# 56 instead of 48 tokens by gathered expert rows, the choice of experts begun earlier, and one comparison for both one-hots

## What is computed

```python
q = (xb @ w_q).reshape(T, 8, 2, 128)                 # the query projection, 2048 x 2048
sc = einsum('thcd,hckd->thck', q, sub_keys)          # 8 heads, 2 halves, 128 keys each
s1, i1 = top_k(sc[:, :, 0], 16); s2, i2 = top_k(sc[:, :, 1], 16)
cand = s1[..., :, None] + s2[..., None, :]           # 256 candidates for each head
best, ci = top_k(cand.reshape(T, 8, 256), 16)
idx = i1[ci // 16] * 128 + i2[ci % 16]               # 128 picks of a token, of 16384 experts
g = softmax(best)
act = gelu(einsum('td,thkd->thk', xb, u_tab[idx]))
out = einsum('thk,thkd->td', g * act, v_tab[idx])
```

## Time and profile before

| | |
|---|---|
| median of 3 timed runs | 1776.24 us (1774.4 to 1777.46) |
| the profiled execution | 1771.97 us, its span 1769.7 us |
| TensorE busy (PE) | 1744.7 us, 99% of the span |
| TensorE's weight loads (PEld) | 1655.2 us |
| VectorE busy (DVE) | 1423.8 us, 80% |
| ScalarE busy (ACT) | 931.9 us, 53% |
| GpSimd busy (POOL) | 415.8 us, 23% |
| DMA | 462.59 MB, mean 261 GB/s |
| high products u, v | 438.4 and 438.9 us busy, 2048 each |
| query projection, u stage, v stage begin | 360, 450 and 1125 us |

### The profile page before, as it was taken

One profiled execution on the slowest core, in us unless ns is written; L12 is line 12 of the kernel. 1 busy time (PEld: TensorE's weight loads), 2 busy tenths in 40 slices (PEclk: granted clock), 3 DMA queues, 4 the chain that ended last, 5 costly groups with the idle time before them and its releaser, 6 DMA issues. The chain is left out here.

```text
span 1769.7 us, 28855 instructions
## 1 busy us (share of the span) xinstructions
PE 1744.7 (99%) x10950; PEld 1655.2 (94%) x10950; DVE 1423.8 (80%) x2151; ACT 931.9 (53%) x1403; POOL 415.8 (23%) x293
## 2 busy tenths in 40 slices
PE   9999999999999999999999999999999999999997
PEld 7887778788999999999999999999999999999997
DVE  4556786575589899999999998688888888888995
ACT  5454574444456555555555545555555545555553
POOL 0002300020142133111111112023434433343341
PEclk9999999999999999999999999999999999999998
DMA  7765455678577677777777779899999999999992
GB/s 233 213 188 167 143 150 178 184 255 236 172 218 219 218 256 243 253 240 230 230 227 228 232 232 324 254 338 373 353 357 344 356 325 356 360 368 403 366 347 85
DMA packets 127138, 462.59 MB, mean 261 GB/s; under 512 B 14864, under 2 KB 14944, under 8 KB 126352
## 3 DMA queue, kind: packets, MB, share of 16 engines
q1 hardware_dynamic: 95760, 347.65, 60.5%
q0 software_dynamic: 30960, 112.64, 17.1%
q10 hardware_dynamic: 288, 0.55, 0.1%
HBM read 455.73 MB, written 5.05 MB: 260 GB/s over the span
## 5 line engine op out<-in xcount | busy, mean ns | idle before, releaser
L1641 PE MATMUL PS<-W,HI 128*128 128x416 f32 x2048 | 438.9, 354 | 1.4 <-DVE W L1222 0.8
L1601 PE MATMUL PS<-xT,HI 128*128 128x416 f32 x2048 | 438.4, 356 | 0.0
L682 ACT ACTIVATE HI<-V_RAW 128x1024 fp32r<-128x1024 f32 x256 | 271.7, 1062 | 282.6 <-PE PS L1641 151.4
L1641 PEld LDWEIGHTS PS<-W,HI 128*128 128x128 f32 x2048 | 366.1, 189 | 7.2 <-DVE OUTA L1256 1.9
L1601 PEld LDWEIGHTS PS<-xT,HI 128*128 128x128 f32 x2048 | 366.0, 189 | 2.9
L1146 DVE TENSOR_TENSOR V_LO<-V_RAW,HI 128x2048 fp32r<-128x2048 f32 x128 | 293.0, 2289 | 48.6 <-ACT HI L682 43.4
L682 ACT ACTIVATE HI<-RING_RAW 128x1024 fp32r<-128x1024 f32 x256 | 269.6, 1053 | 77.5 <-DMA RING_RAW<-u_t 72.0
L1153 DVE TENSOR_TENSOR RING_LO<-RING_RAW,HI 128x1024 fp32r<-128x1024 f32 x232 | 274.4, 1219 | 4.6 <-ACT HI L682 4.6
L819 DVE TENSOR_TENSOR LO<-RAW,HI 128x1024 fp32r<-128x1024 f32 x132 | 163.1, 1238 | 142.8 <-PE PS L1349 97.9
L1607 PEld LDWEIGHTS PS<-xT,RING_LO 128*128 128x128 f32 x2048 | 268.0, 191 | 3.7 <-DVE RING_LO L1153 2.2
L1646 PEld LDWEIGHTS PS<-W,V_LO 128*128 128x128 f32 x2048 | 269.4, 191 | 1.9 <-DVE V_LO L1146 0.8
(11 more groups left out here) (209 smaller groups left out, 1656.9 us busy)
## 6 DMA issues: line engine op xcount, KB each, us to landing
RING_RAW<-u_t SPq DMA_DIRECT2D x256, 512.0 KB
V_RAW<-peer_v SPq DMA_DIRECT2D x256, 512.0 KB
RAW<-w_in SPq DMA_DIRECT2D x80, 512.0 KB, 3.7
RAW<-w_out SPq DMA_DIRECT2D x32, 512.0 KB, 4.4
RAW<-wq_t SPq DMA_DIRECT2D x32, 512.0 KB, 4.8
x_spill<-X POOLq DMA_DIRECT2D x2, 1024.0 KB, 5.8
X1R<-x_spill POOLq DMA_DIRECT2D x8, 256.0 KB
X<-x SPq DMA_DIRECT2D x3, 512.0 KB, 8.4
```

The costliest lines, as they stand in the source:

```text
L682: nc.scalar.activation(HI[:, n % HI_SLOTS, :], raw_of(n), ACT.Copy).then_inc(top_ready, 1)
L1601: return mm(PS[:, j % S_BANKS, 0:2 * ND].rearrange("p (a t) -> p a t", a=2), HI[:, n % HI_SLOTS, kk * P:(kk + 1) * P], xT[:, k, :, 0:ND], ...
L1641: return mm(PS[:, V_BANKS[i], 0:2 * ND].rearrange("p (a t) -> p a t", a=2), HI[:, v % HI_SLOTS, i * P:(i + 1) * P], weights_of(v), start=v ...
```

## The change

- NB_ goes from 16 to 24, so 56 tokens go by gathered rows and ND is 200. A gather of part B now brings 5 picks of 24 tokens (120 of 128 partitions used, the indices of the other 8 zero), so GROUPS_B is 26 and HALVES 232. 65 halves stand in the u stage (two of three spreading steps have one, and the steps after them 1.5 on average), 167 in the v stage. Their order is now dots A, sums A, dots B, sums B, with gelu for each part.
- The choice begins in the query projection: TensorE makes the scores of a pair of heads' halves there (`pair_scores`), ACT copies them out, and VectorE does the first 12 pieces at every second unit. The pieces end in step 47 and spreading begins in step 51, with 50 batches. The loops of the query projection on ACT, VectorE and TensorE are written out. VectorE waits for the saved rows of XS before that loop.
- The one-hots are one comparison on VectorE (ONE, both indices), and the gate is multiplied in on ACT by four activations (`gates_into`), which stand ahead of `put_gates` on ACT. On VectorE `one_hots(b + 1)` now stands ahead of `apply_gates(b)`. `land` keeps its waits.
- Some tiles move (X8, ACC8, PICKED2, PK4), and POOL has low parts in 16 units instead of 24.

```diff
-NA, NB_ = 32, 16
+NA, NB_ = 32, 24
-GROUPS_A, GROUPS_B = P * NA // P, P * NB_ // P
+PICKS = PH * TOPK
+ROWS_A, ROWS_B = P // NA, P // NB_
+PB = ROWS_B * NB_
+GROUPS_A, GROUPS_B = PICKS // ROWS_A, -(-PICKS // ROWS_B)
...
+EARLY = 12
+CHOICE0 = 1
...
-SPREAD0 = 60
+SPREAD0 = PICKS_AT[1] + 2
...
-HALF_STEPS = list(range(40, SPREAD0, 3)) + list(range(SPREAD0, SPREAD_END, 2)) + list(range(SPREAD_END, NKEYS - 7))
+HALF_STEPS = sorted([j for j in range(SPREAD0 - 3, SPREAD_END) if j % 3] + list(range(SPREAD_END, NKEYS - 7))
+                    + list(range(SPREAD_END, NKEYS - 7, 2)))
...
+def half_of(k):
+
+    if k < A_SUMS:
+        return k < A_DOTS, k % A_DOTS // 2, k % 2
+    return k < B_DOTS, GROUPS_A + (k - A_SUMS) % (2 * GROUPS_B) // 2, k % 2
...
+            def pair_scores_out(q):
+
+                act.wait_ge(sc_done, q + 1)
+                nc.scalar.activation(SC[:, TILE_ORDER[0], 2 * q:2 * q + 2, :],
+                                     PS[:, 4 + q % 4, q // 4 * 2 * NKEYS:(q // 4 + 1) * 2 * NKEYS]
+                                     .rearrange("p (a b) -> p a b", b=NKEYS), ACT.Copy).then_inc(sc_out, 1)
+
+            for m in range(4, N_WQ):
+                hi(WQ0 + m)
+                if m >= 9 and m % 4 == 1:
+                    pair_scores_out((m - 9) // 4)
...
+            def gates_into(b):
+
+                act.wait_ge(compared, b + 1)
+                for i in range(TOKB):
+                    t = b * TOKB + i
+                    ins = nc.scalar.activation(ONE[:, 1, i, :], ONE[:, 1, i, :], ACT.Copy, scale=EG[:, 2, t:t + 1])
+                ins.then_inc(ones, 1)
...
+                if 0 <= j + 1 - SPREAD0 < N_BATCH:
+                    gates_into(j + 1 - SPREAD0)
                 if 0 <= j - SPREAD0 < N_BATCH:
                     put_gates(j - SPREAD0)
...
+            dve.wait_ge(xs_saved, 16)
+            for m in range(2, N_WQ + 2):
+                if m < N_WQ:
+                    lo(WQ0 + m)
+                c = (m - 3) // 2
+                if m % 2 and c >= 0:
+                    dve.wait_ge(used, WQ0 + 2 * c + 2)
+                    add_halves(QTQ[:, c, :], c % 2)
+                if m % 2 == 0 and 0 <= (m - 8) // 2 < EARLY:
+                    piece()
...
-                v.tensor_tensor(ONE1[:], IOTA[:].unsqueeze(1).broadcast_to([P, TOKB, NKEYS]),
-                                EG[:, 0, b * TOKB:(b + 1) * TOKB].unsqueeze(2).broadcast_to([P, TOKB, NKEYS]), ALU.is_equal)
-                for i in range(TOKB):
-                    t = b * TOKB + i
-                    ins = v.tensor_scalar(ONE2[:, 4 * i:4 * i + 4, :], IOTA[:].rearrange("p (q c) -> p q c", q=4),
-                                          EG[:, 1, t:t + 1], EG[:, 2, t:t + 1], ALU.is_equal, ALU.mult)
-                ins.then_inc(ones, 1)
+                t0 = b * TOKB
+                v.tensor_tensor(ONE[:], IOTA[:].unsqueeze(1).unsqueeze(1).broadcast_to([P, 2, TOKB, NKEYS]),
+                                EG[:, 0:2, t0:t0 + TOKB].unsqueeze(3).broadcast_to([P, 2, TOKB, NKEYS]), ALU.is_equal)\
+                    .then_inc(compared, 1)
...
-                if 0 <= b < N_BATCH:
-                    apply_gates(b)
                 if 0 <= b + 1 < N_BATCH:
                     assert done == [PIECES, PIECES]
                     one_hots(b + 1)
+                if 0 <= b < N_BATCH:
+                    apply_gates(b)
                 if b >= 0:
                     land(j)
```

250 lines of the change are left out of this document (126 added, 124 removed).

## The result

The changed kernel took 1826.33 us (median of 4 runs, 1818.87 to 1843.52), the kernel before 1775.32 beside it (4 runs, 1772.08 to 1777.46): a ratio of 1.0303, 95% interval 1.0228 to 1.0377. It is 3.0% slower; the forecast was 0.6% slower, 1786, with a range up to 1806. The profiled execution took 1825.0 us (span 1823.2), 53.5 us of span more than the one of before. Ratios are taken without runs in the slower state that some executions fall into, and can differ a little from the quotient of the medians.

What follows compares the result with a forecast made beforehand. TensorE was taken as the bound, with VectorE and DMA close behind. Columns -27.3, batches -1.7, spreading +33 and gathers +6 gave +10.0 on 1771.97, so 1782.0; against the timed median, 4.3 higher, 1786 us, range 1760 to 1806.

Steps and rivals of the forecast that it cites:

- The columns: TensorE, u and v stages: 16 columns fewer in 4096 high products save 27.3 us; 8 fewer in low products, nothing.
- The gap rule: TensorE's isolated gap of N / 2.4 + 2.5 ns; would shorten the low products too, making the sum 13.7 us better.
- The batches: Spreading in the u stage: two batches fewer (52 to 50) at 0.83 us each save 1.7 us.
- The spreading step: u stage: landing waits for ACT's scalings and `put_gates`, so a step takes 6.33 us against TensorE's 5.61; loss 33 us.
- the lead: TensorE's head start in the spreading steps: a batch's gates are ready before its spread wants them, so 2.9 us are absorbed.
- The choice in the query projection: 12 of 82 pieces move into the query projection, with VectorE busy 41 of 50 us there; cost taken as nothing.
- The end of the u stage: Gathered halves at 1.5 per step, VectorE at 4.57 of 4.72 us; 0 to 5 us for late loads, taken as 0.
- The gathers in the v stage: Round trip of 10.06 us against 10.1 available: 0.05 us per pair, 6 us in all; bounds 0 and 39.
- Rival 3: The gather round trip sets the v stage too: at 10.8 us, 39 instead of 6, time 1819; at 10.4, 1796; chance 0.14.

Runs made afterwards that it cites:

- The swap: The changed kernel with `put_gates` ahead of the four scalings on ScalarE in a spreading step, not behind them: 1803.68 us, ratio 1.0183.
- the cut chain: The changed kernel; VectorE applies gates before comparing for the next batch, ScalarE copies gates and low half out before scaling: 1784.75 us, ratio 1.0057.

## Why the forecast was wrong

- **The columns** (-27.3, upper end 13.7 more): measured -34. The high products saved what was taken. The low ones, taken to be at a floor, fell by 0.01 us per 8, and the unit by 0.066 instead of 0.053. The gap rule that the forecast weighed (the Trainium skill, TensorE: Matmul & The Clock Gate, Back-to-back issue gap) would have made it 0.080, as an estimate; the rows lie halfway.
- **The batches** (-1.7): two are gone, and nothing in the runs speaks against their 0.83 us each.
- **The spreading step** (+33): right in mechanism, 9 us short in size. ACT's scaling costs 0.295 us start to start (taken 0.29), the step 6.43 (taken 6.33) against 5.59 (taken 5.61): 0.84 x 50 = 42. Of the 9 us, 6 are the longer step and 3 the lead. The lead is used up after three steps (TensorE first waits at 727.3); it was taken off at 2.9 us, and the mean of 6.43 already has it. The swap and the cut chain show that it is the order and nothing else.
- **The choice in the query projection** (0): 0 by its own run, 93.1 us with and without. VectorE is busy 39.56 of 50 us there, where 41 was forecast. The query stage's +4.3 us are about 3 of pair scores that moved there from the u stage and a slow first unit (its first 7 high products took 3.08 us at 360.62, where the window of 355 to 365 us had a granted clock of 0.83). But the early choice has a price that the forecast did not see, further on: it moves the gathers' dense stretch.
- **The end of the u stage** (0, bounds 0 to 5): 7.0 us of stalls and 2.8 at the slower clock behind the last spread, where before had none, so +10. The forecast added up VectorE's load there (4.57 of 4.72) and asked neither what ScalarE waits for nor what the gathers do at 1.5 per step. ScalarE's gelu, in order ahead of the high parts, waited for the last dot product (a stall of 2.95 us and the slow clock), and VectorE's low parts came late, since VectorE itself waited 9.9 us for rows.
- **The gathers in the v stage** (+6, bounds 0 and 39): this is the step that failed. The stage lost 25.7 us in stalls and 8.0 at the slower clock against 3.3 before, so +30. The forecast read a round trip of 10.06 us off one place of the trace of before, compared it with the 10.1 that the change leaves, found the two about equal and took the small end, 0.05 us per pair. The reading was near the mean, 10.1 us before and after. The step from it to the price was wrong: a mean round trip that equals the spacing is not just covered, since a single one takes from 8.8 to 11.9 us (eight of ten in the changed kernel) and the long ones make VectorE wait. Part of the scatter is the issue on GpSimd, 0.94 us or up to 3.0 behind VectorE's operation in course, part the landing (6.2 to 8.1 us from the end of the issue, again eight of ten). Before, 11.6 us of spacing covered most of it. And VectorE, at 4.39 of 4.716 us by the forecast's own sum, has too little time in hand to catch up, so its waits reach TensorE: 49.7 us for rows of the sums, 21.2 us of TensorE's stalls for value weights behind them. Rival 3 had this as its mechanism (gathers set the v stage, deciding above 10.1 us) at a chance of 0.14, and gave it as an alternative to the spreading loss, while the two add up: 1786 with 30 for 6 and 42 for 33 is 1819, and the end of the u stage (+10) and the columns (-7) bring it to 1822, the measured 1826 less what has no name.

Of the Trainium skill, SBUF — State Buffer (Who interferes with whom) says that an operation of VectorE with two inputs in SBUF and an instruction of GpSimd that reads SBUF exclude each other for the whole of it. The trace agrees for gathers, which read their list there: the issue at 1311.52 ends 0.83 us after the low pair that had begun before it. Whether an issue in turn holds up VectorE these rows don't show. The same section infers that such an operation does not hold up the writing of descriptors for a transfer; for plain transfers no run here was made to show it, for gathers the rows above speak against it.

What stays open: why gathers into 64 or 96 partitions make both queues and the issues slower, and how much of the changed kernel's spread of run times (1818.87 to 1843.52) comes from stalls that tip the clock. How large the cost of the gelu's place is, when the same lines take between 130.7 and 135.2 us from run to run. Of the 53.5 us some 5 in the v stage have no name. Whether the changed kernel's v stage is bound to lose 30 us each time isn't known either: the same lines took 647.2, 646.5, 646.1 and 656.5 us in four traces.

## What to carry to other kernels

A ring with n places asks for a round trip under n times the spacing, and that holds for its long trips, not for its mean: read many of them, and how they scatter, before pricing a smaller spacing, and ask whether the engine that waits has time in hand. Here a spacing equal to the mean cost 30 us, and 10% fewer transfers in the stage gave it back. When work moves to another engine, follow what is queued behind it there: the same operations in another order were worth 41.6 us. And a mean over long and short steps says nothing where the short ones can't give back.

## What the runs showed of the hardware

- A gather's issue on GpSimd takes 0.94 us alone and otherwise ends 0.82 us after VectorE's operation in course (126 of 135 in the v stage), so up to 3.0 behind a low pair of 2.28 us; some lose more than one turn (4.43, and 6.82 with 64 rows).
- A gather of 128 rows of 4 KB beside a stream of tiles at about 350 GB/s lands 8.2 to 8.3 us after the start of its issue (medians after and before); eight of ten land 6.2 to 8.1 us after its end in the changed kernel.
- Gathers of 96 rows of 4 KB took 3.8 us of all DMA engines per MB, those of 128 rows 2.7, and the tiles beside them 3.5 instead of 2.8. Halving the bytes by columns made the changed kernel 29 us faster, halving them by rows 101 us slower.
- TensorE's granted clock fell from 2.4 to 1.2 GHz behind five of the stalls in the v stage, of 1.80, 1.84, 1.85, 2.15 and 5.15 us: the next 8 products of 400 columns took 2.5 to 3.0 us instead of 1.64. It did not fall behind others of 1.94, 2.13 and 2.19 us. It cost 8.0 us there besides 25.7 of stalls.
